# A hybrid retention and state-space layer: mask in the spread matmul, feature-major norm, another planner and beginning

## What is computed

```python
h = x + hybrid_mixer(rmsnorm(x, norm_mix_w), ...)
y = rmsnorm(h + squared_relu_mlp(rmsnorm(h, norm_mlp_w), w_up, w_down), norm_final_w)

# hybrid_mixer: one projection, split into retention q k v g (4 heads of 256)
# and SSD z, x B C, dt (16 heads of 64, 2 groups, state 128), chunks of 128
scores = einsum(q, k) * decay_intra            # retention inside a chunk
state  = chunk_decay * state + kv              # and from chunk to chunk
xbc    = silu(causal_depthwise_conv(xbc))      # SSD
a_cs   = cumsum(dt * a)                        # inside each chunk
L      = exp(where(causal, a_cs[l] - a_cs[s], -inf))
y_diag = einsum(cb, L, x * dt)                 # cb = C B^T
state  = exp(a_cs[-1]) * state + einsum(B, exp(a_cs[-1] - a_cs), x * dt)
# both normed and gated, concatenated, one output projection
```

## Time and profile before

| | |
|---|---|
| median of 3 runs | 1742.88 us (1741.87 to 1743.29) |
| the profiled execution | 1744.06 us |
| its span (first to last instruction, slowest core) | 1742.5 us |
| spans of the 8 cores | 1732.3 to 1742.5 us |
| busy: TensorE, VectorE, ScalarE | 96%, 40%, 23% |
| loads and stores | 155 MB, mean 89 GB/s |

### The profile page before, as it was taken

One profiled execution on the slowest core, in us unless ns is written; L12 is line 12 of the kernel. 1 busy time (PEld: TensorE's weight loads), 2 busy tenths in 40 slices (PEclk: granted clock), 3 DMA queues, 4 the chain that ended last, 5 costly groups with the idle time before them and its releaser, 6 DMA issues.

```text
span 1742.5 us, 26674 instructions; the slowest of 8 cores (1732.3 to 1742.5 us)
## 1 busy us (share of the span) xinstructions
PE 1668.5 (96%) x10410; PEld 968.8 (56%) x10410; DVE 697.6 (40%) x1295; ACT 406.5 (23%) x767; POOL 60.6 (3%) x118
## 2 busy tenths in 40 slices
PE   1789999999999999999999999999999999999997
PEld 1678887766657677644444444444444444444443
DVE  1365765667766555536622121221121221212225
ACT  3333322567652222202211000110001100011013
POOL 0000000000000000000000000000000000000000
PEclk9899999999999999999999999999999999999999
DMA  9727436042326513752554325443244433444424
GB/s 203 213 56 138 113 74 107 4 74 50 74 53 142 97 32 67 122 170 49 97 97 73 73 54 102 83 76 70 52 97 78 82 64 67 97 73 76 85 58 169
DMA packets 23307, 155.13 MB, mean 89 GB/s; under 512 B 2704, under 2 KB 2960, under 8 KB 5904
## 3 DMA queue, kind: packets, MB, share of 16 engines
q0 software_dynamic: 16416, 116.10, 37.1%
q1 hardware_dynamic: 6768, 37.33, 6.3%
HBM read 261.13 MB, written 8.39 MB: 155 GB/s over the span
## 4 chain that ended last, share of the span: by engine, by line
PE 92%; DMA 3%; DVE 1%; issue 1%; ACT 1%; another core or an unknown queue 1%; SPq 0%; DVEq 0%; ACTq 0%; POOLq 0%
PE psum L452 90%; PE psum L455 2%; DMA arena<-xp 2%; DMA arena<-w_ret 2%; ACT arena L473 1%; DVE arena L480 1%; DVE arena L489 0%; SPq L442 0%; DVE arena L484 0%; ACT L473 0%; DVEq L311 0%; DVEq L330 0%; ACTq L330 0%; POOLq L330 0%
## 5 line engine op out<-in xcount | busy, mean ns | idle before, releaser
L452 PE MATMUL psum<-arena 128*128 128x512 bf16 (+6 forms) x9674 | 1635.3, 331 | 23.2 <-DVE arena L480 13.9
L452 PEld LDWEIGHTS psum<-arena 128*128 128x128 bf16 (+1 forms) x9674 | 921.6, 99 | 714.1 <-issue 29.8
L480 DVE TENSOR_TENSOR arena<-arena 128x512 bf16<-128x512 f32 (+6 forms) x351 | 190.7, 550 | 379.6 <-ACT arena L473 370.9
L473 ACT ACTIVATE arena<-psum 128x512 f32<-128x512 f32 (+3 forms) x234 | 130.6, 565 | 786.2 <-PE psum L452 767.1
L480 DVE TENSOR_TENSOR arena<-arena,psum 128x512 f32<-128x512 f32 x190 | 130.0, 687 | 368.1 <-PE psum L452 367.7
L473 ACT ACTIVATE arena<-arena 128x512 bf16<-128x512 f32 (+3 forms) x211 | 158.8, 766 | 412.0 <-DVE arena L489 170.0
L480 DVE TENSOR_TENSOR arena<-psum,arena 128x512 f32<-128x512 f32 (+4 forms) x250 | 174.9, 730 | 159.2 <-PE psum L452 138.0
L489 DVE SCALAR_TENSOR_TENSOR arena<-psum,arena 128x512 f32<-128x512 f32 (+1 forms) x164 | 112.6, 695 | 49.7 <-ACT arena L473 38.5
L473 ACT ACTIVATE arena<-psum,arena 128x128 f32<-128x128 f32 (+3 forms) x212 | 91.4, 508 | 120.2 <-PE psum L452 98.7
L455 PE MATMUL psum<-arena 128*128 128x128 bf16 x736 | 59.3, 228 | 42.1 <-DVE arena L484 36.6
L455 PEld LDWEIGHTS psum<-arena 128*128 128x128 bf16 x736 | 50.9, 103 | 50.3 <-issue 43.6
(11 more groups left out here) (15 smaller groups left out, 15.6 us busy)
## 6 DMA issues: line engine op xcount, KB each, us to landing
arena<-w_up POOLq DMA_DIRECT2D x32, 1024.0 KB, 10.1
arena<-w_down POOLq DMA_DIRECT2D x32, 1024.0 KB, 8.6
arena<-w_ret POOLq DMA_DIRECT2D x22, 1024.0 KB, 10.1
arena<-xm SPq DMA_DIRECT2D x16, 1024.0 KB, 9.0
arena<-xp SPq DMA_DIRECT2D x8, 1024.0 KB, 39.5
arena<-w_xs POOLq DMA_DIRECT2D x8, 1024.0 KB, 10.5
arena<-w_out POOLq DMA_DIRECT2D x8, 1024.0 KB, 10.1
y<-arena SPq DMA_DIRECT2D x14, 512.0 KB, 3.2
```

Source lines behind the costliest of these rows:

```text
L452: P.op("pe", lambda e: e.matmul(R(out), lhsT=lhsT, rhs=rhs, start=start, stop=stop), [lhsT, rhs], [out], c, lat=163.0)
L473: P.op("act", lambda e: e.activation(out=R(out), in_=R(in_), func=func, **kw), ins, outs, c, lat=0.0, table=table)
L480: P.op(eng, lambda e: e.tensor_tensor(out=R(out), in0=R(a), in1=R(b), op=op), [a, b], [out], dcost(out, True), lat=0.0)
```

## The change

**Mask.** The identity matmul with `negm` is gone. `asp` gets 16 more rows (96 to 111, loaded as constants): row 96 + b holds -30000 where a token's block of 8 inside its chunk is before block b; `SEL` gets the matching rows, one where the row's own block is b. So the spread matmul adds -30000 for pairs of blocks above the diagonal. Inside the blocks on the diagonal nothing is masked; there `main` clamps L at 1e30 before multiplying by C B^T, which is zero above the diagonal.

**Norm of the main half.** A second copy of xm, feature-major (`xmt`, two halves of 512 tokens, four quarters of 512 features each), is loaded, 8 loads of 1 MiB more. `square_m` takes the row sums from token-major x, one chunk at a time through one buffer. `root_m` takes four roots at once and spreads them with four float matmuls into one PSUM bank, a row factor per token column. `scale_m` multiplies four feature tiles of a quarter by norm weight and row factor, straight to `xnM`. No transposes, no bf16 copy.

**Planner.** Operations that touch PSUM and are not TensorE's get a rank 1000 places earlier among those that can start at once. Loads are modelled as two queues that share 330 GB/s at 1 to 1.4, with a start of 1.5 us (SP) and 4 us (POOL) and a landing of 1.5 us.

**Beginning and weave.** Head 1's value slab comes right after head 0's; head 0's keys later. In the chunk loop run the values of heads 0 and 1 and the conv tiles of block 0 of both first slabs; all keys move into the weave. The rope tables and the large constants are issued behind the prior x chunks; the identity comes from the first constants by a copy. Main norm, `v0_main`, `dtM` and the first unit's `prod` are all in one weave with the prior rest. `SEL` is loaded, and the diagonals are made, after that weave. The position of `acrep` moves.

```diff
+        rank = list(range(len(recs)))
+        for ops in self.vops:
+            for i in ops:
+                if recs[i]["eng"] != "pe":
+                    rank[i] = i - AHEAD
...
-            if r["dma"]:
-                c0 = max(st + 1200.0, chan)
-                chan = c0 + r["nbytes"] / DMA_RATE
-                fin[i] = chan + 1500.0
+            if r["dma"]:
+                advance(st, False)
+                dq[e].append([r["nbytes"], i, st + DMA_START[e]])
...
-    need("pk0", w_ret[0], [16, 256])
-    for what in ("pb0", "pk1", "pv1", "px00", "px01", ...
+    for what in ("pv1", "pb0", "px00", "pk0", "pk1", "px01", ...
...
-    dma("pool", CB[:, 0:128], cstb[:, 0:128])
+    feed(2)
     dma("sp", CST[:, 0:C_SMALL], cst[:, 0:C_SMALL])
...
+    for c in range(1, 6):
+        xl.append(load_x(c, xp, xst[c]))
+    cp(identb, ident)
...
-        if c == 2 or c == 3:
+        if c < 4:
             feed(1, [xl[c]])
-        if c == 3:
+        if c == 2:
+            dma("sp", p_cos.rearrange("p a b -> p (a b)"), rope_p[:, 0, :])
+            dma("sp", p_sin.rearrange("p a b -> p (a b)"), rope_p[:, 1, :])
             dma("sp", CST[:, C_SMALL:C_END], cst[:, C_SMALL:C_END])
-        if c == 4 or c == 5:
-            load_x(c - 4, xm, xs_)
+        if c == 4:
+            load_x(0, xm, xs_)
+        if c == 5:
+            load_xt(0, 0)
...
+    def square_m(c):
+        act(xb[0], xbuf[0], AF.Square, scale=2048.0 ** -0.5, accum=ssm[c // 4][:, c % 4:c % 4 + 1])
+        if c < 7:
+            load_x(c + 1, xm, xbuf[0])
+    def root_m(hf):
+        r = newton(ssm[hf], EPS, 4)
+        p = bank("T")
+        for k in range(4):
+            mm(p[:, k * 128:(k + 1) * 128], r[:, k:k + 1].to_broadcast([128, 128]), ident, True, True)
+        rowr[hf] = p
+    def scale_m(hf, g):
+        src = xbuf[1].rearrange("p (k t) -> p k t", k=4)
+        for k in range(4):
+            dc = g * 4 + k
+            stt(xnM[:, dc, 4 + hf * 512:516 + hf * 512], src[:, k, :], nw[:, dc:dc + 1], rowr[hf], ALU.mult, ALU.mult)
+        if (hf, g) != (1, 3):
+            load_xt(hf + (g + 1) // 4, (g + 1) % 4)
...
         norm_p(c)
         if c % 2 == 1:
-            head0[c - 1]()
-            head0[c]()
+            v0[c // 2]()
+            v1[c // 2]()
         if c == 3:
             group0[0]()
-            for k in range(4):
-                head1[k]()
+            group0[3]()
...
-    weave(head1[6:] + retP(2) + retP(3), group0[1:] + ssdP(1), ([(lambda c=c: norm_m(c)) for c in range(8)], 0.05, 0.95))
+    weave((rest, 0.0, 0.95), (group0[5:] + ssdP(1), 0.0, 0.85), (main_in, 0.03, 0.85),
+          ([dtM], 0.9, 0.9), (prod(0), 0.9, 1.0))
+    dma("pool", SEL.rearrange("p h n -> p (h n)"), cstb[:, B_SEL:B_END])
...
-                mm(p, identb, negm, True, False)
                 for hh in range(4):
                     h = g * 8 + q * 4 + hh
-                    mm(p[:, hh * 128:(hh + 1) * 128], SEL[0:96, h, :], asp[0:96, c * 128:(c + 1) * 128], False, hh == 3)
+                    mm(p[:, hh * 128:(hh + 1) * 128], SEL[:, h, :], asp[:, c * 128:(c + 1) * 128], True, True)
...
-            tt(M, Ls[c], cbs.unsqueeze(1).to_broadcast([128, 8, 128]), ALU.mult)
+            stt(M, Ls[c], 1e30, cbs.unsqueeze(1).to_broadcast([128, 8, 128]), ALU.min, ALU.mult)
```

More of the change, by code:

```diff
@@ L24 @@
 DMA_RATE = 330.0
+DMA_SHARE = {"sp": 1.0, "pool": 1.4}
+DMA_START = {"sp": 1500.0, "pool": 4000.0}
+DMA_LAND = 1500.0
 TABLE_NS = 1350.0
+AHEAD = 1000
 RESERVE = {"A": 1, "B": 2, "C": 2, "L": 1, "T": 1, "Y": 1}
@@ L203, in schedule, with event @@
         free = {e: 0.0 for e in self.ENG}
-        chan = 0.0
+        dq = {"sp": [], "pool": []}
+        dnow = [0.0]
+        def event(q, now):
+            live = [k for k in q if q[k] and q[k][0][2] <= now]
+            rate = {k: DMA_RATE * DMA_SHARE[k] / sum(DMA_SHARE[x] for x in live) for k in live}
+            times = [now + q[k][0][0] / rate[k] for k in live]
+            times += [q[k][0][2] for k in q if q[k] and q[k][0][2] > now]
+            if not times:
+                return None
+            t = min(times)
+            done = None
+            for k in live:
+                q[k][0][0] -= rate[k] * (t - now)
+                if q[k][0][0] <= 1e-3 and done is None:
+                    done = q[k].pop(0)[1]
+            return t, done
@@ new lines, in landing, with settle @@
+        def landing():
+            q = {k: [list(x) for x in dq[k][:3]] for k in dq}
+            now = dnow[0]
+            while True:
+                got = event(q, now)
+                if got is None:
+                    return None
+                now = got[0]
+                if got[1] is not None:
+                    return now + DMA_LAND
+        def settle(i):
+            for s in succ[i]:
+                se = recs[s]["eng"]
+                same = se == recs[i]["eng"] and not recs[i]["dma"]
+                at = beg[i] + recs[i]["cost"] if same and se == "pe" else fin[i] + XLAT[se]
+                rtime[s] = max(rtime[s], at)
+                indeg[s] -= 1
+                if indeg[s] == 0:
+                    ready[se].append(s)
@@ new lines, in advance @@
+        def advance(limit, one):
+            while True:
+                q = {k: [list(x) for x in dq[k]] for k in dq}
+                got = event(q, dnow[0])
+                if got is None or got[0] > limit:
+                    if got is not None and limit > dnow[0]:
+                        live = [k for k in dq if dq[k] and dq[k][0][2] <= dnow[0]]
+                        for k in live:
+                            dq[k][0][0] -= DMA_RATE * DMA_SHARE[k] / sum(DMA_SHARE[x] for x in live) * (limit - dnow[0])
+                    dnow[0] = max(dnow[0], limit) if limit < 1e17 else dnow[0]
+                    return
+                dq.update(q)
+                dnow[0] = got[0]
+                if got[1] is not None:
+                    fin[got[1]] = got[0] + DMA_LAND
+                    settle(got[1])
+                    if one:
+                        return
@@ L270, in schedule @@
                         freeat[k] = max(fin[x] + XLAT["pe"] for x in self.vops[v])
[L271 to L277, removed]
+            if not r["dma"]:
+                settle(i)
+        while landing() is not None:
+            advance(1e18, True)
         self.sim_ns = max(fin)
@@ L571, in build_program @@
     need("v0", w_v0, [16, 272])
-    need("pk0", w_ret[0], [16, 256])
-    for what in ("pb0", "pk1", "pv1", "px00", "px01", "pk2", "pv2", "pb1", "px10", "pk3", "pv3", "px11"):
+    for what in ("pv1", "pb0", "px00", "pk0", "pk1", "px01", "pk2", "pv2", "pb1", "px10", "pk3", "pv3", "px11"):
         n = int(what[2])
@@ L894, in build_program @@
     r1 = alloc([1024], F32)
+    acrep = alloc([8, 96], F32)
+    spot(pos_x + 12288)
     mid = alloc([1024], BF16)
```

119 lines of the change are left out of this document (57 added, 62 removed).

## The result

The changed kernel takes 0.9846 of the time before, 95% interval 0.9827 to 0.9866: about 1716 us beside 1743.1 us (its profiled execution 1716.61 us, forecast 1711 us, range 1699 to 1731 us). The median over all its executions, 1791 us, is not used here, because in two of them all cores of one die ran at a lower granted clock and took longer; the ratios leave such executions out.

The account below looks back on a forecast made before the run. TensorE's instructions bound the dense stretch, bytes the opening. Terms 10.5 + 11 + 3 + 1 + 5 + 4 = 34.5 us, less 2 us for the load chain, took 32.5 us off 1744.06 us: forecast 1711 us, range 1699 to 1731 us.

Parts of the forecast that it names:

- The opening: Up to 125 us: 39 us of TensorE idle time instead of 50.0, gain 11 us, ends 0 and 19 us.
- rival 5: Better, below 1699 us, if the order uses nearly every opening byte and the clock stays up; chance 0.05.
- The planner's prices: Planner's load model: 1 MiB on the pool queue lands in about 8.7 us, where the old one said 5.9 us.
- Waits for slabs: Two TensorE waits for retention slabs, together 5.4 us, shrink by 3 us (0 to 5.4).
- rival 1: Main half's serial x loads, six per half, come 10 to 20 us late: 1722 to 1735 us; chance 0.15.
- The rank: PSUM-freeing work first wins 1 us of the 2.9 us idle from 350 to 500 us; lower end -3 us.
- The seam: Between the halves: dt chain woven with projections and convs, 5 us of 7.0 us idle go; none if slab late.
- TensorE's work: Decay mask matmuls save 6.9 us, main-half norm transposes 7.1 us, added float matmuls cost 3.5 us: net 10.5 us.
- The clock: Half-clock parts near 70 to 80, 150 to 155, 302 to 315 us lose 7 us; 4 us return (0 to 7).
- Rival 3: Opening runs cold: TensorE bursts between waits from 13 us on start at half clock, 1721 us; chance 0.10.

Follow-up runs that it names:

- The x-first version: Changed kernel with norm by transposes, second slab waiting for x chunk 2, head 1's values later, new load prices: 0.9705 of the kernel before, about 1692 us.

## Why the prediction was right, and where it was not

The time came within 0.3% of the forecast and well inside its range. Several terms were wrong, and their errors cancelled; that the number is this close is in part luck.

- **The opening** (11 us; ends 0 and 19): 12.5 us on the slowest core, with the first transposes at 13.1 us and 37.5 us idle where 39 us were forecast. The last x chunk landed at 66.9 us, where 66 us were taken. The size was right, the owner only half: the prediction argued with the order in which bytes come, but on the kernel before the planner alone gave 9.1 us. The other 3.4 us are left for the new loads and the new order of values, if the parts add up, which was not tried. (A slip that hardly counts: the seven transposes of 16 are 6.2 us by rows 6, not 7 us.) Bytes could have given much more: putting x ahead of the second slab, with head 1's values later, took another 9 us of idle time out. The end of 19 us ("the order uses everything") and rival 5 had such a gain in sight, but from the order of work and not from another order of loads.
- **The planner's prices** were misread. A slab is 2 MiB of float32 in DRAM, 1 MiB of bf16 only where it lands, and the planner counts the former: 11.9 us in the new model and 9.1 us in the old one, not 8.7 and 5.9 us. Slabs land in 8.5 to 9 us alone and in a median of 11.2 us. So the new model was late where the step took it to be close, and correcting its start and share gave 6.6 us.
- **Waits for slabs** (3 us): the waits named so are gone, 5.4 us. In their place came 9.6 us from 125 to 250 us, which are gone with the norm by transposes; the prediction took only 2 us back for them. This is rival 1, and what it said of the mechanism held: six loads in series per half, squares behind quarters on the sync queue, and slow loads of 12 to 17 us among quick ones of 5 to 6 us. Eight quarter loads took 8.8 us in the median:

```profile
DMA to landing us min/median/max: 4.8/8.8/17.3
```

  Rival 1 took the median of the kernel before, 7.2 us, for each of twelve links and so let the chain end 145 us after the first load. The twelve links took 103 us together, 8.6 us each, and the last quarter landed at 261.0 us, 185 us after the first chunk landed at 75.9 us. So 17 of the 40 us of lateness are slower loads, and the other 23 us are waits for engines, for buffers and for the queue's order beyond the 59 us that the rival gave them. The mis-sized term is the chain's: with all that comes of it, clock included, the feature-major norm cost 13 us net where the sum had 1.6 us of gain. The Trainium skill's page "DMA: Bandwidth & Descriptors" (section "Queues, rings and completion order"), whose turns between queues spoke for this rival, agrees with these landings in kind: 15.9 us for a quarter load where others took 5.6 us. It gives no time for them.
- **The rank** (1 us, lower end -3): worth 5 us (0.5 to 9.5 us by the two intervals). The prediction looked only at the 2.9 us of idle time that the kernel before had from 350 to 500 us. That was the wrong row: the question was how much idle time the new, shorter decay stretch would have without it, and that is 6.4 us from 250 to 475 us, against 2.5 us with it.
- **The seam** (5 us): the idle time there went from 7.0 to about 1 us, as forecast, but undoing the weave costs 20 us in this kernel.
- **TensorE's work** (10.5 us): the 32 matmuls and 128 transposes are gone, and the 512-column form went from 5438 to 5406 records and from 1192.4 to 1180.6 us. The float matmuls took 2.1 us, not 3.5 us: their price had been read in a stretch at a mean clock of 0.64 (rows 7, at 301.8 us). The 16 records of the 96-column form, whose work did not change, fell from 2.8 us to 1.9 us. With 6.9 and 7.1 us for what is gone that makes 11.9 us, and busy time fell by 12.1 us, so the two agree, as the clock gave nothing on the slowest core. (By form the sums are rougher: the 512-column form alone fell by 11.8 us, and the 4.9 us over the price of 32 matmuls are not explained.)

```profile
L519 PE MATMUL psum<-arena 128*128 128x512 bf16 x5406 | 1180.6, 379 | 0.5 <-ACT arena L540 0.5
L522 PE MATMUL psum<-arena 128*128 128x128 bf16 x608 | 48.4, 224 | 29.0 <-ACT arena L540 15.9 <-DVE arena L551 13.1
L519 PE MATMUL psum<-arena 128*96 128x128 f32 x16 | 1.9, 272 | 0.0
```

  and in the kernel before, around its float matmuls:

```profile
301.80:306.20 4.40, 4.38 (x22) 0.64 0.88 182
```

- **The clock** (4 us): nothing on the slowest core, which stood at half for 27.3 us where the slowest core before stood 23.9 us; in the mean of the cores 27.3 us became 20.1 us, worth 3.6 us at most, so the term is right for the mean and wrong for the core that decides. (Rows 8 lack a fourth place of the kernel before, 96.7 to 100.1 us.) The places moved from the seam to the load chain:

```profile
42.00:49.00 7.00, 4.93 (x34) 0.65 1.06 231
62.00:70.00 8.00, 4.28 (x26) 0.66 0.96 295
...
158.00:165.00 7.00, 4.08 (x27) 0.66 0.99 180
175.00:179.00 4.00, 2.79 (x17) 0.78 0.89 152
```

  Each fall comes after or in a wait of 2 to 4 us. Rival 3 (a cold opening) did not decide: of the first 125 us 16 us are on record at half, where before it were 14 us, besides the first 32 transposes, which cost some 2 us more than at full speed. The rival's counter-argument, a clock of 1.00 over the first 40 us, rested on a stretch without a record: the transposes of the kernel before took 3.57 us for 32 there, twice the price of rows 6. On the page "TensorE: Matmul & The Clock Gate" of the Trainium skill (section "HAM oscillation — how this bites in real kernels"), which has bursts between waits start at the lower clock, the trace agrees in kind: the transposes behind the waits of 13.1 and 10.8 us took 117 ns each. The x-first version has only 0.4 us of idle time from 40 to 125 us and 2.6 us at half, both in the mean.

## What to carry to other kernels

Where an order is made by a planner, each edit has two effects, its own price and a new order, and the second could be as large as the first here (9.4 us for a removal priced at 6.9, nothing for putting it back): test an edit in its final surroundings, and undo it there. A version of an operation that saved the bound engine 5 us of work but made its data arrive through a serial chain of loads with one buffer cost this fixed order more than it saved: count the links, add up what loads take while others run beside them, and not the median, and add the waits between the links. Read a price only in a stretch at full clock. In an opening that is bound by bytes, ask for each load how many microseconds of work it unlocks for its transfer time, and issue in that order.

## What the runs showed of the hardware

- Beside each other, x chunks on the sync queue came every 8.6 us (1 MiB) and slabs on the pool queue every 9.0 to 9.4 us (2 MiB read, 1 MiB written) in the changed kernel's opening. The quickest of them take 4.8 and 8.7 us from issue to landing. Of the engines' time over the first 60 us the sync queue's packets take 38.6% and the pool queue's 58.1%.
- A float matmul of 128 by 128 by 128 takes 0.24 to 0.26 us at full clock in the changed kernel (two records each), and 0.33 us for the three at the head of the dt chain (six records, 1.0 us, in the run with the norm by transposes). The 0.35 to 0.53 us of rows 6 were read where the clock was at half in part (0.64 in the mean).
- Waits of 2 to 4 us on TensorE went with stretches at half clock whose cost was not small beside that of the waits: in the run with the norm by transposes, with 12.7 us less idle time before 250 us on the slowest core, the clock stood at half for 10.2 us instead of 27.3 us, which is worth up to 8.5 us.
- The clock column is no evidence where the trace has no record: the first transposes took 112 to 117 ns each under a clock of 1.00 in the column, and 56 ns later.
